# Retention in a two-block transformer: the heads' work set between the gate units

## The reference

```python
proj = h @ w_in                       # q, k: 1024 each, v, g: 2048 each
q, k = rotate(q, cos, sin), rotate(k, cos, sin) * dk ** -0.5
# causal, in chunks of 128, with a decay per head:
inner = ((q @ k.T) * decay) @ v       # and the state carried between chunks
o = inner + cross
mu, var = mean(o), mean((o - mu) ** 2)          # over a head's 512 values
o = (o - mu) * rsqrt(var + LN_EPS)
y = (silu(g) * o) @ w_o               # 2048 rows of w_o
```

## Time and profile before

| | |
|---|---|
| median of three runs | 3227.07 us |
| the profiled execution | 3225.99 us |
| its span, first to last instruction | 3223.9 us |
| mean granted TensorE clock | 0.957 |
| TensorE matmuls, weight loads busy | 92%, 82% |
| VectorE, ScalarE busy | 65%, 46% |
| DMA mean over the span | 161 GB/s |

### The profile page before, as it was taken

How to read it: one execution, slowest core, us unless ns; L and a number is a source line. 1 busy time by engine, 2 the same in 40 slices (tenths; PEclk the granted TensorE clock), 3 DMA queues, 4 the chain that set the end, 5 groups by cost and what they waited for, 6 DMA issues and landing times.

```text
span 3223.9 us, 54246 instructions
## 1 busy us (share of the span) xinstructions
PE 2971.4 (92%) x18082; PEld 2637.8 (82%) x18082; DVE 2083.7 (65%) x3950; ACT 1487.0 (46%) x2826; POOL 60.5 (2%) x118
## 2 busy tenths in 40 slices
PE   5898999989999789999999999888889999999998
PEld 4678878778889579999988888765689999988886
DVE  3325895458965658888976666224268888966665
ACT  0103454234543234447975555103244448965554
POOL 0000110001100000000000000000000000000000
PEclk9899999999999899999999999986899999999999
DMA  5135984459954244554245665450145553256563
GB/s 165 56 103 172 303 321 118 131 153 347 347 170 143 79 137 162 182 182 137 99 141 191 193 194 165 135 116 1 27 150 182 182 180 113 98 170 193 192 194 118
DMA packets 318588, 519.29 MB, mean 161 GB/s; under 512 B 40865, under 2 KB 219425, under 8 KB 317858
## 3 DMA queue, kind: packets, MB, share of 16 engines
q1 hardware_dynamic: 302082, 457.83, 45.0%
q0 software_dynamic: 16416, 60.30, 5.1%
HBM read 517.02 MB, written 1.05 MB: 161 GB/s over the span
## 4 chain that ended last, share of the span: by engine, by line
PE 82%; ACT 7%; DVE 5%; issue 3%; DMA 2%; ACTq 1%; SPq 0%; DVEq 0%
PE ps L880 29%; PE ps L808 10%; PE ps L812 10%; PE ps L809 10%; PE ps L783 3%; PE ps L742 2%; PE ps L857 2%; DMA tile_ring<-mlp_w_in 2%; ACT spread L1681 1%; PE ps L753 1%; ACT spread L1687 1%; PE ps L766 1%; ACT hot_pair L1681 1%; PE ps L1336 1%; PE ps L1288 1%
## 5 line engine op out<-in xcount | busy, mean ns | idle before, releaser
L808 PE MATMUL ps<-x_high,w_high 128*128 128x256 f32 x3200 | 799.4, 287 | 44.7 <-ACT w_high L1490 25.7
L809 PE MATMUL ps<-x_low,w_high 128*128 128x256 f32 x3200 | 790.7, 284 | 0.0
L808 PEld LDWEIGHTS ps<-x_high,w_high 128*128 128x128 f32 x3200 | 618.4, 193 | 50.3 <-ACT w_high L1490 28.3
L1832 DVE TENSOR_TENSOR w_low<-tile_ring,w_high 128x512 fp32r<-128x512 f32 x688 | 472.2, 693 | 271.1 <-ACT w_high L1530 179.9
L809 PEld LDWEIGHTS ps<-x_low,w_high 128*128 128x128 f32 x3200 | 619.0, 193 | 0.1
L812 PE MATMUL ps<-x_high,w_low 128*128 128x256 f32 x3200 | 450.8, 284 | 0.0
L880 PE MATMUL ps<-w_high,x_high 128*128 128x512 f32 x1376 | 426.9, 392 | 19.9 <-DVE x_low L1827 19.9
L880 PE MATMUL ps<-w_high,x_low 128*128 128x512 f32 x1376 | 425.9, 391 | 0.0
L880 PE MATMUL ps<-w_low,x_high 128*128 128x512 f32 x1376 | 425.8, 391 | 0.0
L1661 ACT ACTIVATE w_high<-tile_ring 128x1024 fp32r<-128x1024 f32 x256 | 269.8, 1055 | 314.6 <-PE ps L812 314.2
L812 PEld LDWEIGHTS ps<-x_high,w_low 128*128 128x128 f32 x3200 | 414.8, 193 | 0.0
(11 more groups left out here) (321 smaller groups left out, 3270.8 us busy)
## 6 DMA issues: line engine op xcount, KB each, us to landing
tile_ring<-peer_u SPq DMA_DIRECT2D x256, 512.0 KB, 3.2
tile_ring<-peer_v SPq DMA_DIRECT2D x256, 512.0 KB, 4.3
arena<-mod_w POOLq DMA_DIRECT2D x112, 512.0 KB, 6.5
tile_ring<-mlp_w_in SPq DMA_DIRECT2D x64, 512.0 KB, 5.5
tile_ring<-mlp_w_out SPq DMA_DIRECT2D x64, 512.0 KB, 6.5
tile_ring<-ret_w_in SPq DMA_DIRECT2D x48, 512.0 KB, 3.9
tile_ring<-peer_w_q SPq DMA_DIRECT2D x32, 512.0 KB, 4.0
tile_ring<-sb_w_qkv SPq DMA_DIRECT2D x24, 512.0 KB, 4.5
```

The costliest lines, as they stand in the source:

```text
L808: nc.tensor.matmul(dst, cols, x_high[:, c, :], start=c == 0, stop=False)
L809: nc.tensor.matmul(dst, cols, x_low[:, c, :], start=False, stop=False)
L1832: return V.tensor_tensor(w_low[:, k % 2, cols], tile_ring[:, k, cols], w_high[:, k % 2, cols].bitcast(F32), ALU.subtract)
```

## The change

The column stage keeps the eight Q/K units. The eight gate units are written out one by one, and seven steps of head work stand between them: step s (before gate unit s) holds the values of head s-2, the scores of head s-1, the sums of squares of head s-4 and the sums of head s-3. Scores go to bank 4, values to banks 5 and 6, sums to the two halves of bank 7. ScalarE copies the values out of PSUM (VectorE before), takes the squares (VectorE before), the square roots, and the silu of one head at a time, heads 0 to 2 after its last rounding for the gates. VectorE has the decay, centring and scaling beside the gate units, and after the last low part the last head's scaling, three gated products, and the copy of the last gate unit. The output projection's chunks 4h to 4h+3 wait for head h alone. The silu and the gated product of the last head stand inside its first tiles. On SP only the count of units changes.

```diff
-                        ("cross1", 6), ("mlp1", 16), ("retention", 16), ("groups", 12), ("route0", 18),
+                        ("cross1", 6), ("mlp1", 16), ("retention", 8), ("gates", 8), ("route0", 18),
...
-            split_columns(16)
-            all_taken()
-            pe.wait_ge(values_taken, 12)
-            for h in range(RET_H):
-                u = open_unit()
+            split_columns(8)
+            def head_scores(h):
                 for kb in range(2):
                     for c in range(2):
                         n = 2 * h + c
-                        mm = nc.tensor.matmul(bank(u)[:, kb * T:(kb + 1) * T - kb * P], KT[:, n, kb * P:(kb + 1) * P],
+                        mm = nc.tensor.matmul(ps[:, 4, kb * T:(kb + 1) * T - kb * P], KT[:, n, kb * P:(kb + 1) * P],
                                               QT[:, n, kb * P:T], start=c == 0, stop=c == 1)
-                mm.then_inc(unit_done, 1)
-                all_taken()
-                for e2 in range(2):
-                    u = open_unit()
-                    for e in range(2):
-                        col = h * RET_DV + (2 * e2 + e) * P
-                        nc.tensor.matmul(bank(u)[:, e * T:(e + 1) * T], VR[:, 0, col:col + P], probT[:, 0, 0:T],
-                                         start=True, stop=True)
-                        mm = nc.tensor.matmul(bank(u)[:, e * T + P:(e + 1) * T], VR[:, 1, col:col + P], probT[:, 0, T:T + P],
-                                              start=False, stop=True, skip_group_check=True)
-                    mm.then_inc(unit_done, 1)
-            all_taken()
-            for h in range(RET_H):
-                if h:
-                    wait_operand()
-                sum_over(oT, range(4 * h, 4 * h + 4))
-            for h in range(RET_H):
-                squares([range(4 * h, 4 * h + 4)])
+                mm.then_inc(ret_scored, 1)
...
+            def between_gates(s):
+                if s == 1:
+                    all_taken()
+                    pe.wait_ge(values_taken, 12)
+                if 2 <= s <= 5:
+                    pe.wait_ge(ret_decayed, s - 1)
+                    if s > 2:
+                        pe.wait_ge(ret_lifted, 2 * (s - 2))
+                    head_values(s - 2)
+                if 1 <= s <= 4:
+                    head_scores(s - 1)
+                if 4 <= s <= 7:
+                    pe.wait_ge(ret_squared, s - 3)
+                    if s > 4:
+                        pe.wait_ge(ret_deviated, s - 4)
+                    mm = head_sums(sq, s - 4, T)
+                if 3 <= s <= 6:
+                    pe.wait_ge(ret_lifted, 2 * (s - 2))
+                    mm = head_sums(oT, s - 3, 0)
+                if 3 <= s <= 7:
+                    mm.then_inc(ret_summed, 1)
+            def gate_unit(q):
+                u = open_unit()
+                for a in range(2):
+                    at = split.up()
+                    column_products(ps[:, u % BANKS, a * T:(a + 1) * T], a, (high_ready, at),
+                                    (low_ready, at)).then_inc((tile_used, unit_done)[a], 1)
+            assert units.n == UNITS["gates"]
+            for q in range(8):
+                between_gates(q)
+                gate_unit(q)
+            pe.wait_ge(ret_deviated, RET_H)
             split_token_rows(2 * C)
...
-            def token_rows(src, count, rows0, cleared):
+            def token_rows(src, count, rows0, cleared, each=None, between=None):
                 n0, r0, m0 = split.n, row_highs.n, halved.n
                 def chunk(k, j):
+                    if each and k % RING == 0:
+                        act.wait_ge(each, j + k // RING + 1)
                     A(x_high[:, k % RING, :], src[:, j * RING + k, :], ACT.Copy).then_inc(row_high, 1)
                 def body(j, begun=True, ahead=True):
@@ -1531,6 +1576,8 @@
                         if not begun and k == 0:
                             act.wait_ge(*cleared)
                             chunk(0, 0)
+                        if not begun and k == 1 and between:
+                            between()
                         if k + 1 < RING or ahead:
                             chunk(k + 1, j)
                 n_it = count // RING
@@ -1721,12 +1768,56 @@
                 token_rows(gates, P, ROWS[f"experts{l}"], (gate_merged, m0 + P - WEIGH_FROM))
-            high_columns(16, UNITS["retention"], opened=behind_values(2 * C, panel))
-            act.wait_ge(unit_taken, UNITS["groups"])
-            A(gT, gT, ACT.Silu).then_inc(silu_ready, 1)
-            for h in range(RET_H):
-                deviation([RET_DV], eps_ln)
-            token_rows(oT, 2 * C, ROWS["retention"], (heads_ready, 1))
+            high_columns(8, UNITS["retention"], opened=behind_values(2 * C, panel))
+            n0, p0, u0 = split.n, pairs.n, UNITS["gates"]
+            def gate_high(k):
+                act.wait_ge(tile_loaded[k % RING], 16 * (n0 // RING + k // RING + 1))
+                if k % 2 == 0:
+                    act.wait_ge(tile_used, p0 + k // 2)
+                else:
+                    act.wait_ge(unit_done, u0 + k // 2)
+                A(w_high[:, k % 2, :], tile_ring[:, k % RING, :], ACT.Copy).then_inc(high_ready, 1)
+            def gate_silu(h):
+                act.wait_ge(unit_taken, u0 + 2 * (h + 1))
+                own = gT[:, 4 * h:4 * h + 4, :]
+                A(own, own, ACT.Silu).then_inc(ret_gated, 1)
+            def beside_gates(s):
+                if 2 <= s <= 5:
+                    h = s - 2
+                    for e2 in range(2):
+                        act.wait_ge(ret_out, 2 * h + e2 + 1)
+                        A(oT[:, 4 * h + 2 * e2:4 * h + 2 * e2 + 2, :], ps[:, 5 + e2, :].rearrange("p (a t) -> p a t", t=T),
+                          ACT.Copy).then_inc(ret_lifted, 1)
+                if 3 <= s <= 6:
+                    h = s - 3
+                    act.wait_ge(ret_centered, h + 1)
+                    A(sq[:, 4 * h:4 * h + 4, :], oT[:, 4 * h:4 * h + 4, :], ACT.Square).then_inc(ret_squared, 1)
+                if 4 <= s <= 7:
+                    h = s - 4
+                    act.wait_ge(ret_summed, s - 2)
+                    at = (h % 2) * T
+                    A(std[:, at:at + T], ps[:, 7, T:2 * T], ACT.Sqrt, bias=eps_ln, scale=1.0 / RET_DV).then_inc(ret_deviated, 1)
+            gate_high(0)
+            gate_high(1)
+            for q in range(8):
+                if q < 7:
+                    gate_high(2 * q + 2)
+                    gate_high(2 * q + 3)
+                    beside_gates(q + 1)
+                else:
+                    for h in range(RET_H - 1):
+                        gate_silu(h)
+            split.up(16)
+            pairs.up(8)
+            act.wait_ge(tile_used, pairs.n)
+            token_rows(oT, 2 * C, ROWS["retention"], (unit_done, u0 + 8), heads_ready,
+                       lambda: gate_silu(RET_H - 1))
             layer_norm(24, high=True)
...
-            def token_rows(src, count, beside=None):
+            def token_rows(src, count, beside=None, opening=None):
                 n0, r0, m0 = split.n, row_highs.n, halved.n
@@ -1832,7 +1923,7 @@
                     return V.tensor_tensor(w_low[:, k % 2, cols], tile_ring[:, k, cols], w_high[:, k % 2, cols].bitcast(F32),
                                            ALU.subtract)
-                def body(j, ahead=True):
+                def body(j, ahead=True, opening=None):
                     for k in range(RING):
                         v.wait_ge(half_high, j * RING + (m0 + k + 1))
                         low(k, slice(0, 512)).then_inc(half_low, 1)
@@ -1842,8 +1933,12 @@
                             chunk(k + 1, j)
                         if beside:
                             beside(k, j)
+                        if opening and k == 1:
+                            opening()
                 chunk(0, 0)
-                with v.Fori(0, count // RING - 1) as j:
+                if opening:
+                    body(0, opening=opening)
+                with v.Fori(1 if opening else 0, count // RING - 1) as j:
                     body(j)
                 body(count // RING - 1, ahead=False)
                 split.up(count)
@@ -2502,9 +2597,7 @@
             split.up(2 * C)
             v.wait_ge(ret_loaded, 16)
-            def rotated_or_gate(i, u):
-                if i >= 8:
-                    return V.tensor_copy(gT[:, 2 * i - 16:2 * i - 14, :], bank2(u))
+            def rotated(i, u):
                 z = bank2(u)
                 wide = [t.unsqueeze(1).broadcast_to([P, 2, T]) for t in (ret_cos, ret_sin)]
                 cs, sn = ret_t[:, 0, :], ret_t[:, 1, :]
@@ -2518,41 +2611,61 @@
                 low(0, 0)
                 lift_side(1)
                 low(1, 0)
-            low_columns(16, rotated_or_gate, looped=False, opened=lift_behind)
-            for h in range(RET_H):
```

(105 more changed lines are left out.)

## The result

| kernel | median, us | runs | range |
|---|---|---|---|
| before | 3227.47 | 4 | 3219.3 to 3228.3 |
| after | 3200.01 | 4 | 3197.9 to 3207.9 |

The changed kernel takes 0.9924 of the time before, with a 95% interval of 0.9912 to 0.9936: 27.5 us less between the medians, 24.5 between the two profiled executions (3225.99 and 3201.45). Predicted was 3207.5 with 3198 to 3216. The sign and the range held; the forecast lay 7.5 us too high, outside the 3205.5 to 3210 that I had given the likeliest case for its own. The stretch that the change touches came out within 0.3 us of its sum. What was off lies outside it.

A forecast was written before the change was run, and what follows sets the result against it. The prediction saw a serial chain of per-head work after TensorE-bound gate units. Terms of 46.08 + 1.54 + 3.16 + 29.52 + 0.12 + 7.0 + 2.0 gave 89.4 us against 108.8, 19.4 less: 3207.5 us, range 3198 to 3216.

The forecast's parts named there:

- seam: Between Q/K and gate units: VectorE rotates before the first gate tile's low part, so TensorE stalls 1.54 us.
- first step: Before the first scores TensorE waits for every unit to be taken, the first gate unit too: 3.16 us stall.
- step seven: At the seventh step of head work TensorE waits for ScalarE's root and VectorE's centring: 0.12 us stall.
- end gap: After the last gate unit TensorE waits 7.0 us for VectorE's queue before the output projection starts.
- clock behind the first gap: After 3.0 us idle before the first scores TensorE's clock falls to half, costing 2.0 us.
- gate units and head matmuls: TensorE work still on the path: 46.08 us of gate units and 29.52 us of scores, values and sums.
- projection: Output projection: same matmuls and DMAs, still starting at half clock, nothing credited from 46.44 us; bounds 0 and 2.9 us.
- Do VectorE and ScalarE keep up?: Beside the gate units: margin over 6 us at step five, 0.12 us stall at step seven; ScalarE not late at the end.
- the rival on the order of waits: ScalarE's wait for a centred head precedes its next rounding, lengthening step seven's stall and VectorE's tail: 3 to 8 us; chance 0.18.
- Unrolling at nothing: Writing the gate units out instead of looping them costs nothing, bounds 0 to 1 us.
- Head by head frees only one head: At the output projection, releasing chunks head by head hides only head 3's product and silu.
- More gain: Clock survives the first gap, or the projection starts at full level: 2.1 to 5.0 us more, 3202.5 to 3205.4; chance 0.2.

The follow-up runs named there:

- the combined kernel: Changed kernel with last heads' scaling and products moved into the projection, early gate low parts, and scores not awaiting the first gate unit's copy; 3193.4 us, ratio 0.9900.
- the repeat: The changed kernel measured and profiled once more, with no edit; 3200.0 us against 3222.0 for the kernel before, ratio 0.9929.
- its copy beside: The changed kernel a third time, unedited, on one chip with the combined one; 3205.8 us, ratio 0.9936 to the kernel before.
- products behind: Changed kernel with the gated products of heads 1 to 3 put behind the low parts of the projection's first three tiles; 3203.0 us, ratio 0.9928.
- seam: Changed kernel with the low parts of gate tiles 0 and 1 ahead of the last rotation again; 3206.9 us, ratio 0.9953.
- all heads: Changed kernel with head 3's silu and product before the projection, which waits for all four heads; 3211.4 us, ratio 0.9965, profiled again at 3208.8.
- scaling behind: Changed kernel with products 1 to 3 and head 3's reciprocal and multiplication spread over the projection's first five tiles; 3199.2 us, ratio 0.9916.
- no first wait: Changed kernel with TensorE's first scores waiting only for the eight Q/K units, not the first gate unit's copy; 3202.5 us, ratio 0.9942.

## Why the prediction was right, step by step

The profile's stretch counts from the completion of the last Q/K unit, the prediction from its issue, 0.16 us earlier; so after is 88.93 + 0.16 = 89.1 where 89.4 stood, and before 108.8 where 108.8 stood. The measured terms are by issue too, from the starts of the rows, and add up to 89.0.

| term | predicted | measured |
|---|---|---|
| seam, with 0.16 | 1.54 | 1.39 + 0.16 = 1.55 |
| first step, with 0.16 | 3.16 | 3.07 + 0.16 = 3.23 |
| step seven | 0.12 | 0.20 |
| end gap, with 0.16 | 7.0 | 6.65 + 0.16 = 6.81 |
| clock behind the first gap | 2.0 (0 to 2.1) | 1.6 and 0.1 in two profiles |
| gate units and head matmuls | 75.6 | 75.6, from the combined kernel: 77.17 + 0.16 less its gap of 1.53 and 0.20 at step seven |
| projection | 46.4 | 46.0, 45.2, 45.7 |

*What stalls TensorE.* Right in place, size and releaser. The 1.6 is the time from the first scores to the values in the kernel after, 1002.91 - 994.23 = 8.68, less 1.32 + 5.76 at full pace; in the repeat it is 998.37 - 991.21 = 7.16, 0.1 over full pace.

*Do VectorE and ScalarE keep up?* Yes; steps two to six show no stall and step seven 0.20 us, so the rival on the order of waits, with its 3 to 8 us, falls. At the end ScalarE is early, as predicted: it idles for 3.33 us before it rounds the projection's first input (17.4 to 20.7 in the prediction), and VectorE's queue is what is late.

*Unrolling at nothing.* Nothing in the stretch is left for it: the other terms add up to the measured length within 0.1 us. No run tests it alone.

*Head by head frees only one head.* Right, 2.9 us in the stretch.

*Clock behind the first gap.* I let the length of the gap decide, 3.0 us being nearer to the row of 3.34 than to that of 2.56, and took one number for what these runs show to be a toss. Gaps of 3.06 or 3.07 us in eight profiles: the clock fell in five (after, its copy beside, products behind, seam, the second profile of all heads) and held in three (the repeat, all heads, scaling behind). From the first scores to the projection, the end gap taken out, the five took 1.5 to 2.7 us longer than the three; the mean over all eight is 1.1 us over a clock that holds. That the first profile came near to my 2.0 is luck.

*More gain* was the rival that came nearest to the whole time, 3200 against its 3202.5 to 3205.4, but for neither of its reasons in the first profile: there the clock fell both behind the first gap and at the projection's start.

*The step that failed* is the silent one: that everything outside the stretch takes its own time again. Between the two profiled executions the time fell by 24.5 us. The stretch gave 19.7, the projection 0.4; the sums of layer norm cost 1.7 (5.42 us for 16 matmuls after, where part of them ran at half clock, 3.73 before); sparse attention gave 6.1, and the other stages cancel. Those 6.1 are chance: the repeat of the same kernel took 119.11 there, as the kernel before did. Since the kernel before ran anywhere from 3210.7 to 3231.3 over all comparisons, and its three runs shown had 3227 as their median, about 20 us are the change's own and the rest of the 27 is, as far as the profiles show, what these executions drew. The two later comparisons bear it out: 22.0 us between the medians on one chip, 18.0 on another. So the forecast's 19.4 us was nearer to the change's own worth than the first comparison was, and that the measured median stayed inside my range owes something to the width I had given it for this scatter. (The sum less the median of three is 3207.7, not 3207.5; nothing hangs on the 0.2.)

What stays open: what decides between the three lengths of the sparse attention, whether the clock falls behind a given gap, and why the medians of the seam and of the version that waits for all heads lie 7 and 11 us above the repeat's. No run here separates these.

## What to carry over

When serial work is moved between units bound by another engine, write each in-order queue's whole tail behind the last unit: here it was all that was left, and it was cut by putting the last products between the next stage's own operands. Price what the rebuilt pieces gain by themselves apart from their overlap with the other stage: here it was 9 of the 21 us in the stretch, which I had expected to be nothing. Judge an edit of a few us by its stretch in the profile, and look at what the untouched stages did before reading a reason out of the total.

## What the runs showed of the hardware

The length of a gap does not settle TensorE's clock. Behind 3.07 us it held or fell, in one kernel; and layer norm's second sums, behind a shorter gap of 1.98 us each time, took 3.72 us at full clock in three of the fourteen profiles (before, no first wait, scaling behind) and 5.41, partly at half, in eleven. TensorE in order of time, first the kernel without the first wait, then the repeat:
```profile
1122.07 3.72 PE L1182 MATMUL ps<-arena,keep 128*128 128x256 f32 x16 [1.98 <-ACT arena L1687]
```
```profile
1122.27 5.41 PE L1182 MATMUL ps<-arena,keep 128*128 128x256 f32 x16 [1.98 <-ACT arena L1687]
```
Before the projection, behind 4.42 us and more it started at half every time (eleven profiles, the kernel before among them), behind 1.37 us it held in all three profiles that have such a gap. The fall need not come during the gap: in the kernel after the granted clock was still 1.00 when TensorE resumed, and fell about 1 us later. By stretch:
```profile
994.00:995.00 1.00, 0.77 (x4) 0.70 (x5) 0.17 (x1) 0.00 (x0) 0.00 (x0) 1.00 0.47 139
996.00:997.00 1.00, 1.00 (x6) 1.00 (x6) 0.56 (x1) 0.00 (x0) 0.00 (x0) 0.50 0.88 260
```
Sparse attention, with a granted clock of 0.62 to 0.67, lasted from 112.9 to 122.1 us in different executions with nothing changed in it, and one kernel alone had both 112.9 and 119.1.
